# Second FFN matrix: Strassen's algorithm (7 block products for 8) on 16 of its 22 row chunks

## The reference

```python
def swiglu(h, w_gate, w_up, w_down):
    return (jax.nn.silu(h @ w_gate) * (h @ w_up)) @ w_down      # 1024 -> 2816 -> 1024
...
        h = rms_norm(x, g_pre_ffn[i])
        x = x + rms_norm(swiglu(h, w_gate[i], w_up[i], w_down[i]), g_post_ffn[i])
```

## Time and profile before

| | |
|---|---|
| time, median of 3 runs | 1331.24 us (1331.05 to 1331.68) |
| profiled execution, its own time | 1331.45 us |
| profiled execution, span from first to last instruction | 1329.7 us |
| PE busy | 1309.0 us, 98% |
| DVE busy | 697.3 us, 52% |
| ACT busy | 555.3 us, 42% |
| POOL busy | 31.3 us, 2% |

### The profile page before, as it was taken

The page is one execution under the profiler, slowest core; times in us unless marked ns, Lnnn a source line. Parts: engine busy times, 40 slices in busy tenths (PEclk is TensorE's granted clock), DMA queues, the critical chain, the costliest instruction groups (busy, mean ns, idle before and its releaser), DMA issues.

```text
span 1329.7 us, 17273 instructions
## 1 busy us (share of the span) xinstructions
PE 1309.0 (98%) x6352; PEld 1089.4 (82%) x6352; DVE 697.3 (52%) x1382; ACT 555.3 (42%) x1161; POOL 31.3 (2%) x67
## 2 busy tenths in 40 slices
PE   9999999999999999999999999999999999999998
PEld 8888887898888888888788888778877788888887
DVE  4388887563332233335765578664544434443444
ACT  4467776443332222323554323554245442322333
POOL 3000000000000000000110000000000000000000
PEclk9999999999999999999999999999999999999999
DMA  6312212123223222222243232112322022232241
GB/s 231 127 49 76 76 45 84 64 83 139 95 96 117 105 95 95 95 95 96 95 159 111 96 127 95 64 44 84 127 70 89 33 96 95 95 111 95 96 157 65
DMA packets 23029, 128.50 MB, mean 97 GB/s; under 512 B 2725, under 2 KB 4901, under 8 KB 9513
## 3 DMA queue, kind: packets, MB, share of 16 engines
q1 hardware_dynamic: 20072, 124.35, 26.4%
q10 hardware_dynamic: 2880, 3.15, 0.7%
HBM read 123.28 MB, written 4.20 MB: 96 GB/s over the span
## 4 chain that ended last, share of the span: by engine, by line
PE 91%; DVE 4%; ACT 2%; issue 2%; POOL 1%; ACTq 0%; POOLq 0%; DVEq 0%
PE bank L1503 27%; PE bank L1505 26%; PE bank L1504 26%; PE ob L1664 4%; PE sc L1644 3%; PE tp L1653 2%; DVE w_lo L945 1%; PE bank L1674 1%; POOL rstd L470 1%; ACT w_hi L514 1%; PE bank L1584 1%; PE bank L1591 0%; PE bank L1598 0%; DVE arena L974 0%; ACT arena L594 0%
## 5 line engine op out<-in xcount | busy, mean ns | idle before, releaser
L1503 PE MATMUL bank<-xT_hi,w_hi 128*128 128x512 f32 (+1 forms) x1136 | 448.2, 395 | 3.2 <-DVE w_lo L945 2.5
L1505 PE MATMUL bank<-xT_hi,w_lo 128*128 128x512 f32 (+1 forms) x1136 | 436.4, 384 | 0.0
L1504 PE MATMUL bank<-xT_lo,w_hi 128*128 128x512 f32 (+1 forms) x1136 | 435.8, 384 | 0.0
L945 DVE TENSOR_TENSOR w_lo<-w_raw,w_hi 128x512 fp32r<-128x512 f32 x424 | 269.2, 685 | 262.9 <-ACT w_hi L514 262.1
L514 ACT ACTIVATE w_hi<-w_raw 128x512 fp32r<-128x512 f32 x424 | 237.1, 621 | 138.3 <-PE bank L1505 129.5
L1503 PEld LDWEIGHTS bank<-xT_hi,w_hi 128*128 128x128 f32 x1136 | 213.9, 188 | 45.1 <-DVE w_lo L945 4.0
L1505 PEld LDWEIGHTS bank<-xT_hi,w_lo 128*128 128x128 f32 x1136 | 213.5, 188 | 42.9
L1504 PEld LDWEIGHTS bank<-xT_lo,w_hi 128*128 128x128 f32 x1136 | 214.0, 188 | 39.6 <-issue 1.2
L522 ACT ACTIVATE arena<-bank 128x512 f32<-128x512 f32 x90 | 53.6, 597 | 210.1 <-PE bank L1505 209.8
L1503 PE MATMUL bank<-w_hi,act_hi 128*128 128x512 f32 (+1 forms) x312 | 121.5, 389 | 0.0
L1505 PE MATMUL bank<-w_hi,act_lo 128*128 128x512 f32 (+1 forms) x312 | 119.8, 384 | 0.0
(11 more groups left out here) (174 smaller groups left out, 1366.8 us busy)
## 6 DMA issues: line engine op xcount, KB each, us to landing
w_raw<-in_weights SPq DMA_DIRECT2D x104, 1024.0 KB, 4.8
x_sb<-in_x SPq DMA_DIRECT2D x4, 512.0 KB, 6.4
w_raw<-in_weights SPq DMA_DIRECT2D x4, 512.0 KB, 8.4
arena<-in_bias ACTq DMA_DIRECT2D x16, 128.0 KB, 2.1
x_dram<-x_sb SPq DMA_DIRECT2D x1, 2048.0 KB, 10.8
x_sb<-x_dram SPq DMA_DIRECT2D x1, 2048.0 KB, 10.6
arena<-cum_dram SPq DMA_DIRECT2D x1, 1024.0 KB, 4.6
out<-arena SPq DMA_DIRECT2D x4, 256.0 KB, 2.1
```

Source lines behind the costliest of these rows:

```text
L945: nc.vector.tensor_tensor(w_lo[b % RING][:, cols], w_raw[b % RING][:, cols], w_hi[b % RING][:, cols].bitcast(F32), ALU.subtract).then_inc( ...
L1503: nc.tensor.matmul(ps, hi_l, hi_r, start=first, stop=False)
L1504: nc.tensor.matmul(ps, hi_l, lo_r, start=False, stop=False)
L1505: return nc.tensor.matmul(ps, lo_l, hi_r, start=False, stop=last)
```

## The change

The 22 chunks are now cut into groups of 8, 8 and 6. Each group of 8 is a quad: its activations are seen as 2 x 2 blocks (two halves of the tokens, 256 each; even and odd chunks, 4 each), its weights as 2 x 2 blocks (even and odd chunks; two halves of the columns, 512 each), and the result is made with 7 block products in the form of Winograd. Each is 24 matmuls of 128x512. The left operands are `a11`, `a12`, `a22` and four sums `s1` to `s4`, which DVE makes with each pair of chunks, 256 elements wide; the right ones are three of the loaded blocks and four sums, which DVE makes in place in the raw buffers (128x2048). Some products are accumulated onto a bank whose earlier content ACT has read out; the rest is added by DVE in SBUF (`fold`), during the gate and up blocks that follow. Two more raw buffers lie in the arena. The last 6 chunks are done as before, in blocks of 3 and 3, and their result is added to the quads'. There are no loops any more on SP, PE, DVE and ACT in this part. The order of ACT and DVE in the norm is the same.

```diff
-FH = FC // 2
+GU = (8, 8, 6)
+QUADS = 2
+QK2 = GU[0] // 2
+ST = S // 2
...
+WHOLE, SUM_1, SUM_2, PLAIN_22, SUM_3, PLAIN_21, SUM_4 = range(7)
+LHS = ("a11", "s1", "s2", "s4", "s3", "a12", "a22")
+LHS_STEP = {"a11": 0, "s3": 1, "s1": 2, "s2": 3, "s4": 4, "a12": 5, "a22": 6}
+QUAD_BANK = (0, 2, 1, 2, 1, 0, 1)
...
-    for f in range(2):
-        add(f"gu{f}", FH, 2 * FH)
-        for h in range(2):
-            add(f"down{f}{h}", 3, TT)
+    for f, count in enumerate(GU):
+        add(f"gu{f}", count, 2 * count)
+        if f < QUADS:
+            first[f"quad{f}"] = n
+            for i in range(len(LHS)):
+                done.append(("quad_full", 2 * (len(LHS) * f + i + 1)))
+            n += len(LHS)
+    for h in range(2):
+        add(f"down{h}", 2, TT)
...
+            loaded(b + WHOLE, 2)
+            loaded((b, "12"), 3)
+            loaded(b + PLAIN_22, 0)
+            loaded(b + PLAIN_21, 1)
+            slot[b + SUM_1], slot[b + SUM_2], slot[b + SUM_3], slot[b + SUM_4] = 2, 2, 3, 1
...
+        w_raw = [w_ring[0][:, :], w_ring[1][:, :], view(9216, BLK), view(9216 + BLK, BLK)]
+        even, odd = g_first[:, 0:S], g_first[:, S:2 * S]
...
+        quad_bank = [[bank[0], bank[1]], [bank[2], bank[3]], [sc[0], sc[1]]]
...
+            def gated_pair(f, p):
+
+                b, e = FIRST[f"gu{f}"] + 2 * p, USE[f"gu{f}"] + 4 * p
+                read_out(sg[:, 0, :], e, ACT.Silu)
+                if f and p == 0:
+                    act.wait_ge(quad_full, 2 * quad_at(f, 0))
+                act.wait_ge(*freed(e + 1))
+                round_lhs(f, p, "a11", "s3")
+                split(b + 2)
+                read_out(sg[:, 1, :], e + 2, ACT.Silu)
+                act.wait_ge(*freed(e + 3))
+                round_lhs(f, p, "s1")
+                if p == QK2 - 1:
+                    split(b + 3)
...
+            def quad_out(f, i, dst):
+
+                for r in range(2):
+                    act.wait_ge(quad_full, 2 * quad_at(f, i) + r + 1)
+                    nc.scalar.activation(dst[:, r, :], quad_bank[QUAD_BANK[i]][r][:, :], ACT.Copy).then_inc(quad_free[QUAD_BANK[i]][r], 1)
+
+            for f in range(QUADS):
+                for p in range(QK2):
+                    gated_pair(f, p)
+                b = FIRST[f"quad{f}"]
+                split(b + SUM_2)
+                if f:
+                    act.wait_ge(folded, 8)
+                quad_out(f, WHOLE, p1_kept)
+                split(b + PLAIN_22)
+                quad_out(f, SUM_1, p5_kept)
+                split(b + SUM_3)
+                quad_out(f, SUM_2, m12_second if f else m_sb[:, 0:2, W:2 * W])
+                split(b + PLAIN_21)
+                split(b + SUM_4)
+                quad_out(f, SUM_3, m22_second if f else m_sb[:, 2:4, W:2 * W])
+                split(b + len(LHS))
+                quad_out(f, PLAIN_21, m11_second if f else m_sb[:, 0:2, 0:W])
+                split(b + len(LHS) + 1)
+                quad_out(f, SUM_4, m21_second if f else m_sb[:, 2:4, 0:W])
...
+            def gated_pair(f, p, folds):
+
+                b, e = FIRST[f"gu{f}"] + 2 * p, USE[f"gu{f}"] + 4 * p
+                n = 4 * (QK2 * f + p)
+                step(folds, 1)
+                gated(e, even, sg[:, 0, :])
+                nc.vector.tensor_tensor(sums["s3"], even[:, 0:ST], even[:, ST:S], ALU.subtract).then_inc(x_summed, 1)
+                split_lhs(f, p, "a11")
+                split_lhs(f, p, "s3")
+                split(b + 2)
+                if p == QK2 - 1:
+                    quad_sum(f, SUM_1)
+                step(folds, 1)
+                gated(e + 2, odd, sg[:, 1, :])
+                nc.vector.tensor_tensor(sums["s1"], even[:, ST:S], odd[:, ST:S], ALU.add).then_inc(x_summed, 1)
+                dve.wait_ge(x_summed, n + 2)
+                nc.vector.tensor_tensor(sums["s2"], sums["s1"], even[:, 0:ST], ALU.subtract).then_inc(x_summed, 1)
+                dve.wait_ge(x_summed, n + 3)
+                nc.vector.tensor_tensor(sums["s4"], odd[:, 0:ST], sums["s2"], ALU.subtract).then_inc(x_summed, 1)
+                split_lhs(f, p, "s1")
+                if p == QK2 - 1:
+                    split(b + 3)
+                    split_lhs(f, p, "s2", "s4", "a12", "a22")
+                    quad_sum(f, SUM_2)
+                else:
+                    split_lhs(f, p, "s2", "s4", "a12", "a22")
+                    split(b + 3)
+
+            def quad_sum(f, which):
+
+                n = 4 * f + (SUM_1, SUM_2, SUM_3, SUM_4).index(which)
+                b = FIRST[f"quad{f}"]
+                if which == SUM_1:
+                    dve.wait_ge(w_loaded[3], 16 * LOADS[b, "12"])
+                    dve.wait_ge(w_split, PARTS * (b + WHOLE + 1))
+                    ins = nc.vector.tensor_tensor(w_raw[2], w_raw[3], w_raw[2], ALU.subtract)
+                if which == SUM_2:
+                    dve.wait_ge(w_loaded[0], 16 * LOADS[b + PLAIN_22])
+                    dve.wait_ge(w_split, PARTS * (b + SUM_1 + 1))
+                    ins = nc.vector.tensor_tensor(w_raw[2], w_raw[0], w_raw[2], ALU.subtract)
+                if which == SUM_3:
+                    ins = nc.vector.tensor_tensor(w_raw[3], w_raw[0], w_raw[3], ALU.subtract)
+                if which == SUM_4:
+                    dve.wait_ge(w_split, PARTS * (b + PLAIN_21 + 1))
+                    ins = nc.vector.tensor_tensor(w_raw[1], w_raw[1], w_raw[2], ALU.subtract)
+                ins.then_inc(w_summed, 1)
...
+            def folds_of(f):
+
+                n = 8 * f
+                for r in range(2):
+                    m12, m21, m22 = m_sb[:, r, W:2 * W], m_sb[:, 2 + r, 0:W], m_sb[:, 2 + r, W:2 * W]
+                    fold(m22, p5_kept[:, r, :], n + 1, (f, SUM_1, r), (f, SUM_3, r))
+                    fold(m21, p1_kept[:, r, :], n + 2, (f, WHOLE, r), (f, SUM_4, r))
+                    yield
+                    fold(m12, p1_kept[:, r, :], n + 3, (f, PLAIN_22, r))
+                    fold(m22, p1_kept[:, r, :], n + 4)
+                    n += 4
+                    yield
...
+            folds = iter(())
+            for f in range(QUADS):
+                for p in range(QK2):
+                    gated_pair(f, p, folds)
+                b = FIRST[f"quad{f}"]
+                split(b + SUM_2)
+                quad_sum(f, SUM_3)
+                split(b + PLAIN_22)
+                split(b + SUM_3)
+                split(b + PLAIN_21)
+                quad_sum(f, SUM_4)
+                split(b + SUM_4)
+                add_p3(f)
+                split(b + len(LHS))
+                split(b + len(LHS) + 1)
+                folds = folds_of(f)
...
-                with pe.Fori(0, GU_LOOP[f][1]) as turn:
-                    for i in range(GU_LOOP[f][0], GU_LOOP[f][0] + 2):
-                        feature_major(FIRST[f"gu{f}"] + i, USE[f"gu{f}"] + 2 * i, 2, KD, xT_hi, xT_lo, turn=turn)
...
+            def quad(f):
+
+                b = FIRST[f"quad{f}"]
+                for e in range(USE[f"gu{f + 1}"] - 4, USE[f"gu{f + 1}"]):
+                    pe.wait_ge(*freed(e))
+                for i, name in enumerate(LHS):
+                    o, where = b + i, QUAD_BANK[i]
+                    opens = where not in QUAD_BANK[:i]
+                    for r in range(2):
+                        if f or not opens:
+                            pe.wait_ge(quad_free[where][r], quad_drained(f, i) - 1)
+                        for k in range(QK2):
+                            if r == 0:
+                                pe.wait_ge(w_split, PARTS * o + k + 1)
+                                pe.wait_ge(lhs_split, lhs_at(f, k if name == "a11" else QK2 - 1, name))
+                            tok = slice(P * r, P * r + P)
+                            last = product(quad_bank[where][r][:, :], lhs_hi[name][:, k, tok], lhs_lo[name][:, k, tok],
+                                           w_hi[o % RING][:, part_columns(k)], w_lo[o % RING][:, part_columns(k)], opens and k == 0, k == QK2 - 1, not opens)
+                        last.then_inc(quad_full, 1)
...
-            token_major(FIRST["down11"], USE["down11"], (4, 4, 3), W, act_hi, act_lo,
-                        after=transposes_at("pre2", {(1, 2, 2): 0, (2, 3, 0): 1}),
-                        order=((0, 0), (0, 1), (0, 2), (0, 3), (1, 0), (2, 0), (1, 1), (2, 1), (1, 2), (1, 3), (2, 2), (2, 3)))
+                if f < QUADS:
+                    quad(f)
+
+            def gated_ready(i, t):
+                if t == 0:
+                    pe.wait_ge(act_split, 3 * (i + 1))
+
+            token_major(FIRST["down0"], USE["down0"], (3, 3), W, act_hi, act_lo, gated_ready)
+            token_major(FIRST["down1"], USE["down1"], (3, 3), W, act_hi, act_lo,
+                        after=transposes_at("pre2", {(1, 2, 0): 0, (1, 3, 1): 1}),
+                        order=((0, 0), (0, 1), (1, 0), (1, 1), (0, 2), (0, 3), (1, 2), (1, 3)))
```

More of the change, by code:

```diff
@@ L129, with places, loaded @@
 FIRST, USE, DONE = plan()
-N_BLOCKS = len(DONE)
+N_OPERANDS = len(DONE)
+def places():
```

(30 more changed lines are left out.)

303 lines of the change are left out of this document (170 added, 133 removed).

## The result

| | before | after |
|---|---|---|
| time, median | 1331.28 us (8 runs, 1331.05 to 1332.31) | 1335.58 us (8 runs, 1335.38 to 1335.90) |
| ratio | | 1.0031, 95% interval 1.0020 to 1.0042 |
| span of the profiled execution | 1329.7 us | 1333.9 us |

What follows compares the result with a forecast made beforehand. PE bounds the kernel before 620 us; from 620 to 648 us a DVE, POOL and ACT chain does. Saved matmuls -6.80 us plus quad entries 2.3 give -4.5: 1326.7 us against the 1331.24 median; 8-in-10 range 1324.2 to 1330.3.

Steps and rivals of the forecast that it cites:

- 0.2267 us for every matmul that stays: Pace per 128x512 matmul, from 48 matmuls in 10.88 us between gate/up blocks; used to price removed and remaining PE work.
- R: Moment the last half of token tile 0 is complete, 619.95 us before the change; forecast to come 4.5 us sooner.
- Rival 3: In the quads, DVE weight sums take over; at 5.4 us a sum, 1335.4 us; chance 0.07.
- The two entries: Each quad's start waits for four banks of the last gate/up blocks: 1.15 us each, 2.3 us for two.
- Only 30 of 48 matmuls count: 18 of the matmuls saved fall behind R and become PE waiting; 30 x 0.2267 = 6.80 us saved.
- Rival 1: All 48 removed matmuls count, PE going on as now behind R: 1322.7 us; chance 0.07.
- The wait forecast at 3.1 us: New PE wait behind R, before tile 1's transposes, for its scaled rows from DVE: about 3.1 us.
- The weight sums: Four 128x2048 DVE sums per quad, beside PE's products, 2.34 us each, hidden and costed at nothing.
- Rivals 2: Quads starve mildly: short DVE and ACT waits cost 0.2 more each, product three 1.1 us late; 1329.2 us; chance 0.12.
- the margins: DVE and ACT slack in a quad: 1.3 us at the third product, 1.8 for third and fourth together.
- Rival 4: The new 3.1 us idle behind R drops PE's clock to half speed: 1330.0 us; chance 0.05.
- Rival 5: The change does not do what it says, for example written-out code fetched late: about 1331 us; chance 0.04.

Runs made afterwards that it cites:

- with 32 bytes: The changed kernel with a 32-byte-per-partition tensor put ahead of act_hi, moving act_hi, act_lo and the arena: 1334.53 us, ratio 1.0022.
- with 160 bytes: The changed kernel with 160 unused bytes per partition ahead of act_hi, so it starts 128 past a multiple of 256 bytes: 1327.43 us, ratio 0.9970.
- 160 bytes without 12 matmuls behind R: The changed kernel with 160 bytes ahead of act_hi, leaving out 12 third-term matmuls of the last down half behind R: 1327.20 us.
- with 96 bytes: The changed kernel with 96 bytes per partition ahead of act_hi, which then starts at a multiple of 64 bytes, not 128: 1332.75 us, ratio 1.0009.
- without 12 matmuls in the quads: The changed kernel with 160 bytes ahead of act_hi, leaving out 12 third-term matmuls, six in each quad's last product, ahead of R: 1324.61 us.

## Why the prediction was wrong, point by point

**What failed: 0.2267 us for every matmul that stays.** The prediction measured that pace on matmuls that read `xT` and `act` at their old places, and carried it over to a layout in which `act` is elsewhere. It never priced the moving of the tensors, and no rival did. That cost stood at nothing, without a reason. It is 1224 x 7.0 ns = +8.6 us, 0.3 of it hidden behind R, against the 1335.58 - 1327.43 = 8.15 measured. Part of it, 4.0 us, falls behind the second block of the next product, where the forecast had no term at all; the conv branches lie 400 us behind the change.

**A number that came true by chance.** Rival 3 ends at 1335.4 us, and 1335.58 was measured. It is a coincidence: its weight sums of 5.4 us are 2.29 us here, and the loss is somewhere else.

**What held.** With the operands back in phase the kernel takes 1327.43 us, where the sum said 1326.7.

- The two entries are there, but each costs more than the 1.15 us of the forecast. The first matmul starts 1.34 and 1.31 us late (364.45 and 492.23 against the starts before them, 362.88 and 490.69, plus 0.227), and is itself 0.08 longer: 2.8 us in all, not 2.3. Taking the wait away gave 2.7 us (3.1 with 32 bytes). What I had too low is the step from DVE to PE: the multiplication ends at 364.09, and PE starts 0.36 us later, where I took 0.06 to 0.14 from PE's waits for a split. Why this one is longer, no run shows.
- Only 30 of 48 matmuls count: shown by the pair of kernels without 12 matmuls (0.2 us and 2.8 us). Rival 1 is out. The wait forecast at 3.1 us is 3.05, and the second block is 24.1 us behind R: in the changed kernel (24.09) and in the one with 160 bytes, where R is 616.14, the next start in the first two rows below:

```profile
615.91 0.39 PE L1737 MATMUL bank<-w_hi,act_lo 128*128 128x512 f32 x1
616.14 0.39 PE L1735 MATMUL bank<-w_hi,act_hi 128*128 128x512 f32 x1
...
640.22 0.50 PE L1735 MATMUL bank<-w_hi,xT_hi 128*128 128x512 f32 x1 [0.95 <-DVE w_lo L1076]
```

  R comes 3.8 us sooner than before, for 4.5 forecast. The entries explain 0.5 of the 0.7. For the rest I have no row; two kernels that are alike up to that point (160 bytes, and 160 bytes without 12 matmuls behind R) reach the first quad 0.6 us apart (363.68 and 363.11), so it is within what one profile can be off. The block products are 5.44 us apart there (369.24 to 374.68), as forecast, and not 5.62.
- The weight sums take 2.29 us (forecast 2.34) and are hidden. Rivals 2 and 3 are out; the price in rival 3 was too high, since the margins are 0.7 us and more larger than reckoned.
- The Trainium skill (VectorE: DVE Perf Modes, "The TRN2 errata") gives 2.29 us for that sum by its formula; the row agrees.
- Rival 4, the clock: right in the fact, wrong in the price. Behind the wait of 3.05 us the granted clock averages 0.57 over 4 us [the window above], that is half speed (1.2 GHz) for most of it; before, it was 1.00 there. The slower transposes and matmuls only use up idle time ahead of the second block, which stays 24.09 us behind R. In two kernels whose clock did not fall there it is the same (616.75 to 640.84 with 96 bytes, 613.06 to 637.14 without 12 matmuls in the quads). It costs nothing here.
- Rival 5 is out: the matmuls are fewer as written, and the written-out loops cost nothing that shows.

## What to carry to other kernels

A change of the memory layout is an edit with a price, even where no instruction changes: compare the mean duration of the matmuls that the change does not touch, by operand, before and after. In this kernel two operands of a matmul of 512 float32r columns should start at the same place modulo 256 bytes of the partition; small tensors belong behind the large ones, or with a pad. And a saved matmul is worth its time only up to the point from which another engine's chain sets the end; leaving a dozen of them out on either side of that point shows where it is.

## What the runs showed of the hardware that was not expected

- TensorE's pace in a stream of weight load and matmul (128x512, float32r, full clock) depends on where the moving and the stationary operand lie against one another: 227 to 228 ns at a difference of 0 modulo 256 bytes, 229.8 at 64, 233 to 234 at 32, 96 to 192 and 224, that is 1 to 3%. Moving all of them by 32 bytes does not matter (1331.23 us). It is alike with the shifted tensor as the moving and as the stationary operand at 128 (233.1 and 232.7), not at 64 and 192, which are the same pair in exchanged roles (229.8 and 233.3). Whether it is the weight load for the matmul itself or for the next one that disturbs, the runs do not tell, since both come from the same tensor; nor which mechanism it is.
- The Trainium skill (TensorE: Matmul & The Clock Gate, "Step-by-step: what each phase is for") says that loading the next tile's weights takes no read bandwidth of SBUF from the running matmul. No run here measures that bandwidth. What the rows show is that the loads take 188 to 189 ns in both kernels, and that the matmuls are up to 7 ns slower where the two operands are out of phase; so the sentence can't be taken to mean that the pace is the same at all addresses.
- Behind its wait of 3.05 us TensorE's clock was at the lower level (1.2 GHz) for a while in the changed kernel (0.57 over 4 us), and so it was in four more profiles with a wait of 3.06 to 3.10 us in the same place (0.57 to 0.66), and behind a wait of only 2.44 us in the kernel without 12 matmuls behind R (0.60, and again behind its next one of 2.28). In three it stayed at 1.00: with 32 bytes behind 3.06 us, with 96 bytes behind 3.09, and without 12 matmuls in the quads behind 3.10. So the length of the wait alone does not decide it. The rows of these three, in that order:

```profile
634.10:638.10 4.00, 3.97 (x22) 3.44 (x23) 3.67 (x6) 0.98 (x3) 0.00 (x0) 1.00 0.22 33
...
631.00:635.00 4.00, 3.94 (x22) 3.42 (x23) 3.70 (x7) 0.96 (x3) 0.00 (x0) 1.00 0.25 39
...
627.30:631.30 4.00, 3.93 (x22) 3.38 (x23) 3.71 (x7) 0.95 (x3) 0.00 (x0) 1.00 0.20 31
```
